# Block-0 modulation slabs by VectorE and TensorE instead of a ring and GpSimd, plain fp32 slabs for the convolution, output tile by tile

## What is computed

```python
mod = c_act @ w_ada[l] + b_ada[l]                 # 1024 x 6144 weights, one row of input
sh1, sc1, g1, sh2, sc2, g2 = jnp.split(mod, 6, axis=-1)
mix = token_mixer(modulate(x, sh1, sc1), ...)
x = layer_norm(DEEPNORM_ALPHA * x + g1[:, None, :] * mix, ln1_g[l], ln1_b[l])
ff = swiglu(modulate(x, sh2, sc2), w_gate[l], w_up[l], w_down[l])
x = layer_norm(DEEPNORM_ALPHA * x + g2[:, None, :] * ff, ln2_g[l], ln2_b[l])

# token_mixer
proj = h @ w_in
q, k, v, qi, ki, wi, gate_b, gate_c, hc = jnp.split(proj, offsets, axis=-1)
attn = sparse_indexer_attention(rope(q), rope(k), v, rope(qi), rope(ki), wi, 64)
attn = group_rms_norm(attn, attn_norm_g, 8)
u = gate_c * hc                                   # then a causal convolution of width 3
conv_out = group_rms_norm(gate_b * conv(u), conv_norm_g, 8)
return concatenate([attn, conv_out]) @ w_out
```

## Time and profile before

| | us |
|---|---|
| median of 3 runs | 1203.74 |
| lowest, highest | 1199.9, 1203.8 |
| the profiled execution | 1200.84 |
| its span | 1199.1 |
| PE busy | 1099.6 (92%) |
| DVE busy | 748.5 (62%) |
| ACT busy | 575.7 (48%) |
| POOL busy | 224.5 (19%) |
| mean granted clock of TensorE | 0.95 |
| end of the last out0 residual | 226.7 |

### The profile page before, as it was taken

The page is one execution under the profiler, slowest core; times in us unless marked ns, Lnnn a source line. Parts: engine busy times, 40 slices in busy tenths (PEclk is TensorE's granted clock), DMA queues, the critical chain, the costliest instruction groups (busy, mean ns, idle before and its releaser), DMA issues.

```text
span 1199.1 us, 20759 instructions
## 1 busy us (share of the span) xinstructions
PE 1099.6 (92%) x8133; PEld 1017.3 (85%) x8133; DVE 748.5 (62%) x1165; ACT 575.7 (48%) x977; POOL 224.5 (19%) x235
## 2 busy tenths in 40 slices
PE   6987575999999989998999999998997899999997
PEld 6686454799999968887999999997875599999997
DVE  5698543767775455774865565576777675655554
ACT  1554251474453446542555445465546664554452
POOL 0030202023331002101133331012220023332001
PEclk9988676989999999998999999998999999999998
DMA  9733406646655526440355545563432056554650
GB/s 352 283 145 141 175 1 211 210 155 215 226 167 164 153 71 233 157 172 1 104 182 206 195 134 172 179 233 141 141 137 75 1 182 204 176 188 124 198 193 36
DMA packets 182451, 192.78 MB, mean 161 GB/s; under 512 B 5673, under 2 KB 142162, under 8 KB 182258
## 3 DMA queue, kind: packets, MB, share of 16 engines
q1 hardware_dynamic: 181376, 191.15, 47.4%
q0 software_dynamic: 144, 0.52, 0.2%
q10 hardware_dynamic: 866, 0.21, 0.1%
HBM read 190.83 MB, written 1.05 MB: 160 GB/s over the span
## 4 chain that ended last, share of the span: by engine, by line
PE 68%; DVE 14%; ACT 7%; DMA 5%; issue 3%; POOL 2%; SPq 1%; POOLq 0%; DVEq 0%; ACTq 0%
PE gemm L1847 20%; PE gemm L1849 19%; PE gemm L1848 19%; DVE wlo L1222 4%; ACT whi L820 2%; DMA raw<-in_w_out 2%; PE gemm L1999 1%; DMA early<-in_w_ada 1%; PE aux L2252 1%; DMA raw<-in_w_in 1%; ACT raw L931 1%; POOL raw L653 1%; DMA raw<-in_gla_w_in 1%; PE aux L1962 1%; DVE xlo L1248 1%
## 5 line engine op out<-in xcount | busy, mean ns | idle before, releaser
L1222 DVE TENSOR_TENSOR wlo<-raw,whi 128x1024 fp32r<-128x1024 f32 (+2 forms) x340 | 386.7, 1185 | 135.5 <-ACT whi L820 134.9
L1847 PE MATMUL gemm<-ohi,whi 128*128 128x256 f32 x1504 | 433.7, 288 | 5.0 <-DVE olo L1248 3.8
L1848 PE MATMUL gemm<-olo,whi 128*128 128x256 f32 x1504 | 426.2, 283 | 0.0
L1849 PE MATMUL gemm<-ohi,wlo 128*128 128x256 f32 x1504 | 426.0, 283 | 0.0
L820 ACT ACTIVATE whi<-raw 128x1024 fp32r<-128x1024 f32 (+2 forms) x340 | 303.7, 961 | 95.9 <-PE gemm L1849 54.8
L1847 PEld LDWEIGHTS gemm<-ohi,whi 128*128 128x128 f32 x1504 | 289.8, 193 | 15.2 <-DVE olo L1248 6.6
L1848 PEld LDWEIGHTS gemm<-olo,whi 128*128 128x128 f32 x1504 | 290.0, 193 | 1.6 <-issue 1.2
L1849 PEld LDWEIGHTS gemm<-ohi,wlo 128*128 128x128 f32 x1504 | 289.5, 192 | 0.0
L1847 PE MATMUL gemm<-acthi,whi 128*128 128x256 f32 x528 | 147.9, 280 | 0.0
L1849 PE MATMUL gemm<-acthi,wlo 128*128 128x256 f32 x528 | 147.5, 279 | 0.0
L1848 PE MATMUL gemm<-actlo,whi 128*128 128x256 f32 x528 | 147.2, 279 | 0.0
(11 more groups left out here) (343 smaller groups left out, 1482.0 us busy)
## 6 DMA issues: line engine op xcount, KB each, us to landing
raw<-in_ffn_w_in SPq DMA_DIRECT2D x44, 1024.0 KB, 6.5
raw<-in_ffn_w_out SPq DMA_DIRECT2D x32, 704.0 KB, 5.3
raw<-in_gla_w_in SPq DMA_DIRECT2D x6, 2048.0 KB, 8.0
raw<-in_diff_w_in SPq DMA_DIRECT2D x6, 2048.0 KB, 7.8
raw<-in_w_gate SPq DMA_DIRECT2D x11, 1024.0 KB, 5.2
raw<-in_w_up SPq DMA_DIRECT2D x11, 1024.0 KB, 7.4
raw<-in_w_down SPq DMA_DIRECT2D x16, 704.0 KB, 5.4
raw<-in_w_ada SPq DMA_DIRECT2D x5, 2048.0 KB, 8.0
```

The lines of the kernel that those rows point to most:

```text
L1222: dve.tensor_tensor(wlo[hslot][:, q * w:(q + 1) * w], raw[slot][:, q * w:(q + 1) * w], whi[hslot][:, q * w:(q + 1) * w].bitcast(F32), ALU. ...
L1847: pe.matmul(dst, st_hi, mv_hi, start=start, stop=False)
L1848: pe.matmul(dst, st_hi, mv_lo, start=False, stop=False)
L1849: return pe.matmul(dst, st_lo, mv_hi, start=False, stop=stop_)
```

## The change

- The slabs `ada4` and `ada5` become part slabs like `ada7` to `ada11` (28 parts in place of 20), `ada6` is loaded whole into the place of `whi0` (`late`) when `in_q`'s tiles are done, and PE sums it by itself in 32 one-column matmuls (`columns_by_c`), eight before and 24 behind the group statistics. `scale_by_c` and `sum_slab` are gone, and with them POOL's part in the modulation.
- `in_gc`, `in_hc` and `in_gb` are "direct": eight plain fp32 matmuls a tile out of the raw slab, no halves by ACT and DVE. Their buffer is free when their four tiles are done.
- SP's order follows: parts stand between the slabs.
- DVE takes parts 4 and 5 between the score heads, 6 and 7 before the first logit, 8 to 11 in heads 0 to 3, and the rest beside `out0` and the feed-forward. The high half of the first operand moves from ACT to DVE; the residual's scaling by ALPHA, the scaling of probabilities and the copy of head pairs move from DVE to ACT. ACT and DVE wait for eight modulations before `out0`.
- At the end PE transposes a residual tile as soon as it is added, ACT copies pairs of tiles, DVE makes the last product in POOL's place and the last copy; SP stores four blocks of 256 columns.

Core of the diff:

```diff
-POOL_SLABS = (4, 5, 6)
-PART_SLABS = (7, 8, 9, 10, 11)
+PART_SLABS = (4, 5, 7, 8, 9, 10, 11)
...
-    ada = lambda i: Phase(f"ada{i}", 1, SLAB, 0, 1, by="pool" if i in POOL_SLABS else "mod", ahead=False,
-                          ring=i not in (2, 3), slot=0 if i == 0 else 1)
-    mixer = lambda name, slot: Phase(name, 1, SLAB, 4, 1, ahead=False, slot=slot)
+    ada = lambda i: Phase(f"ada{i}", 1, SLAB, 0, 1, by="mod", ahead=False, ring=i < 2, slot=i % 2)
+    direct = lambda name, slot: Phase(name, 1, SLAB, 4, 1, by="direct", ahead=False, slot=slot)
...
-        Phase("in_kv", 1, 8 * KV, 0, 1, by="kv", ahead=False, slot=0), mixer("in_q", 1), mixer("in_gc", 0), ada(4),
-        mixer("in_hc", 0), ada(5), mixer("in_gb", 0), ada(6),
-        Phase("out0", 2, SLAB, 4, 1, slot=0), *ffn(0),
+        Phase("in_kv", 1, 8 * KV, 0, 1, by="kv", ahead=False, slot=0),
+        Phase("in_q", 1, SLAB, 4, 1, ahead=False, slot=1), direct("in_gc", 0), direct("in_hc", 1), direct("in_gb", 0), ada(6),
+        Phase("out0", 2, SLAB, 4, 1, slot=1), *ffn(0),
...
+            def load_late():
+                wait(sp, tile_done, PH["in_q"].tile0 + 4)
+                for dst, src in sources["ada6"](0, late):
+                    sp.dma_start(dst, src).then_inc(late_in, 16)
+
             behind = {("ada1", 0): [load_x], ("in_q", 0): [*parts(0, 1), load_const, *parts(2, 3)],
-                      ("ada6", 0): parts(4, 5), ("gate_up0", 0): parts(6, 7), ("gate_up0", 1): parts(8, 9, 10, 11),
-                      ("gate_up0", 2): parts(12, 13), **{("gate_up0", i): parts(10 + i) for i in range(4, 10)},
-                      ("gla_z", 0): [load_gates]}
+                      ("in_hc", 0): parts(4, 5), ("in_gb", 0): [*parts(6, 7), load_late, *parts(8, 9)],
+                      ("out0", 0): parts(10, 11, 12, 13), ("gate_up0", 0): parts(14, 15),
+                      ("gate_up0", 1): parts(16, 17, 18, 19), ("gate_up0", 2): parts(20, 21),
+                      **{("gate_up0", i): parts(18 + i) for i in range(4, 10)}, ("gla_z", 0): [load_gates]}
...
-            for tt in range(TT):
-
-                sp.wait_ge(out_read, 2 * (tt + 1))
-                sp.dma_start(out[0, tt * P:(tt + 1) * P, :], tl(o_tok, tt, w=D)).then_inc(stored, 16)
-            sp.wait_ge(stored, 16 * TT)
+            rows_out = out[0].rearrange("(t p) n -> p t n", p=P)
+            for n in range(4):
+                sp.wait_ge(out_read, n + 1)
+                if n == 3:
+                    sp.wait_ge(last_read, 1)
+                sp.dma_start(rows_out[:, :, 256 * n:256 * (n + 1)],
+                             v3(o_tok[:, :], 2)[:, :, 256 * n:256 * (n + 1)]).then_inc(stored, 16)
+            sp.wait_ge(stored, 64)
```

```diff
-            def sum_slab(i):
-
-                w = raw[PH[f"ada{i}"].slot]
-                me.next(scaled_by_c)
-                me.link(pool.tensor_tensor(w[:, 0:2048], w[:, 0:2048], w[:, 2048:4096], ALU.add))
-                me.link(pool.tensor_tensor(w[:, 0:1024], w[:, 0:1024], w[:, 1024:2048], ALU.add))
-                wait(pool, mod_done, sum_free(i))
-                me.did(pool.tensor_tensor(MOD_SUM[i][:, :], w[:, 0:512], w[:, 512:1024], ALU.add), pool_summed)
...
-            def scale_by_c(i):
-
-                ph = PH[f"ada{i}"]
-                act.wait_ge(landed[ph.slot], ph.landed[0])
-                for k in range(KT):
-                    w = raw[ph.slot][:, 512 * k:512 * (k + 1)]
-                    ins = act.activation(w, w, ACT.Copy, scale=c_act[:, k:k + 1])
...
+            def scale_probabilities(i):
+                act.wait_ge(inverted, i + 1)
+                for qt, (c0, n) in enumerate(((0, P), (P, 2 * P))):
+                    ap = logit[:, 384 * (i % 2) + c0:384 * (i % 2) + c0 + n]
+                    ins = act.activation(ap, ap, ACT.Copy, scale=rsum[:, 2 * (i % 2) + qt:2 * (i % 2) + qt + 1])
+                me.did(ins, prob_ready)
+
+            def take_pair(p):
+                act.wait_ge(pv_done, 2 * p + 2)
+                me.did(act.activation(tl(mixed, p), X[2][:, 0:T], ACT.Copy), attn_ready)
+
...
-                if i in (0, 1):
-                    split_all("in_gb", "in_gc", range(2 * i, 2 * i + 2))
-                if i == 2:
-                    scale_by_c(5)
                 if i in (4, 5):
-                    split_all("out0", "in_hc", range(2 * i - 8, 2 * i - 6))
+                    split_all("out0", None, range(2 * i - 8, 2 * i - 6))
...
+                if i in (2, 4, 6):
+                    take_pair(i // 2 - 1)
+            take_pair(3)
+            group_squares(1, attn_ready, 4)
             group_squares(3, gated_ready, 4)
             group_root(2, G[1])
             prep(order=(0, 1), free=PH["in_gb"].tile0 + 4)
-            group_squares(1, attn_ready, 4)
+            group_root(1, X[1])
             prep(order=(4, 5))
             group_root(3, X[0])
+            prep(order=(2, 3))
             prep(order=(6, 7))
-            group_root(1, X[1])
-            prep(order=(2, 3))
-            scale_by_c(6)
+            wait(act, mod_done, 8)
...
+            for n in range(4):
+                w = 256 if n < 3 else P
+                act.wait_ge(out_done, min(2 * n + 2, KT - 1))
+                act.activation(v3(o_tok[:, :], 2)[:, :, 256 * n:256 * n + w], v3(X[(n + 1) % 4][:, :], 2)[:, :, 0:w],
+                               ACT.Copy).then_inc(out_read, 1)
...
-                me.next(ohi_ready)
+                me.link(dve.tensor_copy(tl(ohi, t), tl(om, t)), ohi_ready)
...
-            me.did(dve.tensor_scalar(res[:, :], res[:, :], ALPHA, None, ALU.mult))
...
-            for q in range(4):
-                low(PH["in_gc"], At(0), q)
+            modulate_part(4)
+            modulate_part(5)
             add_heads(range(4, IH))
...
-                low(PH["in_hc"], At(0), q)
+            modulate_part(6)
+            modulate_part(7)

...
+                invert_sums(i)
                 if i + 1 < NH:
                     masked_maxima(i + 1)
-                for q in {1: (0, 1), 2: (2, 3)}.get(i, ()):
-                    low(PH["in_gb"], At(0), q)
+                if i < 4:
+                    short_conv(i)
+                    modulate_part(2 * PARTS + i)
+                else:
+                    gated_conv(i - 4)
                 for q in {5: (0, 1), 6: (2, 3)}.get(i, ()):
                     low(PH["out0"], At(0), q)
-                if i < 4:
-                    short_conv(i)
-                else:
-                    gated_conv(i - 4)
-                if i in (2, 4, 6):
-                    take_pair(i // 2 - 1)
...
-            take_pair(3)
             me.again(gated_ready)
             prep(mix_make, order=(4, 5))
+            prep(mix_make, order=(2, 3))
             prep(mix_make, order=(6, 7))
-            me.again(attn_ready)
-            prep(mix_make, order=(2, 3))
-            dve.wait_ge(mod_done, 7)
+            dve.wait_ge(mod_done, 8)
+            dve.wait_ge(res_scaled, 1)
+            me.seen(pv_done, NH)
...
+                    if k == 2 and t == KT - 1:
+                        dve.wait_ge(ple_sig, 2 * KT)
+                        me.link(dve.tensor_tensor(tl(prod, t % 2), tl(sg, t % 2), tl(pp, t), ALU.mult))
+                    else:
+                        me.next(ple_prod)
...
             ffn(2)
             ple(2)
-            for n in range(4):
-                me.next(out_done)
-                me.did(dve.tensor_copy(tl(o_tok, n, w=512), G[n][:, :]), out_read)
+            dve.wait_ge(out_done, KT)
+            dve.tensor_copy(v3(o_tok[:, :], 2)[:, :, D - P:D], v3(G[0][:, :], 2)[:, :, 0:P]).then_inc(last_read, 1)
...
+            def columns_by_c(i, src, ks, first, last):
+
+                for k in ks:
+                    for m in range(4):
+                        ins = pe.matmul(X[3][:, 4 * i + m:4 * i + m + 1], src[:, 512 * k + P * m:512 * k + P * (m + 1)],
+                                        c_act[:, k:k + 1], start=k == first and m == 0, stop=k == last,
+                                        skip_group_check=True)
+                return ins
...
+                if not ph.split:
+                    if t == 0:
+                        pe.wait_ge(landed[ph.slot], ph.landed[0])
+                    w = flat(ph.slot, KT, 512)
+                    banks.claim(G[t], freed)
+                    for k in range(KT):
+                        ins = pe.matmul(G[t][:, 0:T], w[:, k, t * P:(t + 1) * P], tl(om, k), start=k == 0, stop=k == KT - 1)
+                    ins.then_inc(tile_done, 1)
+                    return
...
-            modulation(7)
+            modulation(4)
...
-                    modulation(4)
+                    modulation(5)
                 if i == 5:
-                    modulation(5)
+                    modulation(7)
...
+            pe.wait_ge(late_in, 16)
+            columns_by_c(6, late, range(0, 2), 0, None)
+            group_stats((1, 3), C("blk"), mix_sq, (X[1], X[0]))
```

(14 more changed lines are left out.)

79 lines of the change are left out of this document (32 added, 47 removed).

## The result

The changed kernel takes 1184.02 us (median of four runs, 1181.6 to 1185.81) against 1202.57 (four runs) for the kernel before on the same chip: a ratio of 0.984 with the interval 0.982 to 0.986, 18.6 us less. Forecast were 8 us less (1196), with a range that began at 1184: the direction was right, the size was under half of what came.

The account below looks back on a forecast made before the run. The stage up to out0's end was taken as bound by waits. Its − 5 and the tail's − 3 sum to − 8 us: 1193 from the profiled 1200.8, 1196 against the median 1203.7; range 1184 to 1208.

Parts of the forecast that it names:

- The chain of waits: Up to out0's end: DVE waits for parts 6 and 10, and PE's ada6 sum replaces 21 us ahead of out0.
- second stop: In heads 2 and 3, DVE needs parts 10 and 11, issued behind out0's slab: + 4 to + 9, 8 us taken.
- serial line: Ahead of out0, ACT scaling ada6, POOL summing it, then out0's second slab, 173.1 to 194.2 us: these 21 us go.
- parts land early: Rival, chance 0.20: loads share bandwidth and parts come with their slabs, first logit at 97, total 1184 to 1188 us.
- the price of a plain fp32 tile: In in_gc, in_hc and in_gb, a plain tile takes 8 × 0.53 = 4.2 us, against 2.8 for a split one.
- First logit: Start of the heads, 97.2 us before: a DVE wait for parts 6 and 7 puts it at about 103.
- Heads: First logit to in_gb's last tile, 64.4 us before: + 11 − 4.7 − 12 + 8 gives 67, ending at 170.
- Last in_gb tile to last residual: Up to out0's last residual, 64.6 us before: 13 + 1.5 + 35.4 = 50, ending at 220, plus 1.7 added.
- The gate's addition and the warm-up: Between PE's ada6 sum and out0's first tile: 1.5 us.
- the 4.6 us for the lower clock: In out0, two of eight tiles at the lower clock take some 2.3 us more each, added to 8 × 3.85.
- the 1.7 for a standstill: At out0's start, 1.7 us added as three engines start from standstill and ACT has the second slab's high halves first.
- Tail: Behind the last product, fewer late transposes, a smaller copy and DVE's product save 3.5, stores ± 0.5: − 3 us.

Follow-up runs that it names:

- the two runs: Changed kernel with the output written as before: 1188.1 us, 3.8 slower; kernel before with only the new output part: 1199.0 us, 4.1 faster.
- the doubled tiles: Changed kernel with the four plain tiles of one slab computed twice, a run each for in_gc, in_hc and in_gb: 1196.7, 1195.5 and 1197.0 us.

## Why the prediction was wrong

**The chain of waits was right, step by step; three sizes in it were wrong.** `allow` was freed of POOL and of no use, since DVE then waits for part 6: forecast wait 8 to 12 us, measured 8.3. There was a second stop at part 10, no serial line ahead of out0, no POOL row between 80 and 187 us, and the end was 3 us shorter. The parts landed behind their slab, 8.9 us after in_gb's issue, forecast 10. The rival "parts land early" gives the right total, but for a reason that did not occur. The sizes that failed are the price of a plain fp32 tile (4.2 us forecast, 3.46 to 3.65 measured), the second stop (8 forecast, 14 measured), and the start and speed of out0.

**First logit, 103 forecast, 99.8 measured.** PE began in_gc at 73.9, forecast 74. The term is the plain tile: 4 × 0.75 = 3.0 us too much. What else was off cancels: the load took 1.1 less than forecast, DVE's work on the two parts 1.1 more. I divided in_kv's 16.8 us by its 32 matmuls and took the mean for the price of a 128-wide one, though a quarter of them load 40 columns. The Trainium skill, FP8 and Floating Point Precision, section TensorE Precision Notes, gives four passes for true FP32; the estimate from that, with the split tile's measure, is 3.75 us, and the traces have 3.46 to 3.65. I had written that by it the forecast would be lower and kept the row: the page was nearer. Two smaller readings were off without effect on the sum: the top-k began at 72.7, not at 75, hidden behind the wait for part 6; and 406 GB/s is not the best of the earlier trace rows, which shows 417.

**Heads, 67 forecast, 62.5 measured**, and that agreement is in part luck, since two errors offset each other. Without the second stop the heads take 48.3 us (the run with parts 10 and 11 early); the forecast had 59 for that. 4.4 of the 10.7 are the tile's price. The rest, 6, I put down, without a run for it, to work of ACT and DVE that the change took out of the heads (in_gb's halves, the waits behind ada5) and to the lower clock behind the old stop, of which I took only the idle time; the runs don't separate these, and the probabilities are not among them. Against that the stop itself cost 14 to 16 us, not 8, since I let a head cover some of it and left out the clock behind it: PE stood for 11.7 us and then lost 3.1 at half the clock.

**Last in_gb tile to last residual, 51.6 forecast, 47.0 measured.** PE's sum of ada6 ended 13.2 us after the tile, as forecast. Then three terms were off. The gate's addition and the warm-up took 4.0 us, not 1.5. Out0's tiles took 29.8 us from the first matmul (179.5) to the last residual (209.3), not 35.4: in this execution the clock was full from the first of them on, behind the warm-up, so the 4.6 us for the lower clock did not come, and a tile took 3.7, not 3.85. And the 1.7 for a standstill had nothing behind it and nothing came of it.

Summed: 3.2 + 4.5 + 4.6 = 12.3 us too little gain in the stage, all three in one direction. The 4.6 and the 1.7 us were added to be careful, the tile's price was a misreading, and all made the forecast slower; the range should have reached lower.

**Tail.** − 3 forecast, − 2.9 in the trace, 3.8 and 4.1 in the times of the two runs and 3.0 and 2.5 in their traces.

## What to carry to other kernels

A mean over a group of unequal instructions is no price for one of them: look for the rows in a stretch where only the wanted kind runs, or take the shapes apart. A stop of PE costs more than its idle time, because the work behind it starts at 1.2 GHz; here 12.7 us of DVE's waiting, 11.7 of PE's, cost 14 to 16. When small loads stand behind a large one whose issue hangs on a late reader, ask whether they need to: moving two pairs of 512 KB loads by a line, with the late slab behind the first pair, gave about as much again as the whole change (20.7 and 18.6 us). And where two traces begin a stage 3 us apart, compare distances inside them: by distances the doubled tiles cost their whole length, which the times left open.

## What was not expected of the hardware

- A weight load of 40 columns made its matmul record cost 0.375 us where a load of 128 columns has 0.216.
- The clock fell from full to half while PE did one-column matmuls without a break (1.00, 0.58, 0.50 in successive stretches). Two fp32 matmuls of 512 columns, 3.8 us, ran at half the clock, and 1.2 us behind them it was full.
- Behind a like stop the first plain tile took 4.80 us in one execution and 6.31 in another, where it takes 3.65 at full clock.
- An fp32 DVE addition of two SBUF tiles (128x384) took 1.51 us instead of 0.56 beside one POOL product that began 0.2 us before it; it ended 0.4 us after POOL's. The Trainium skill, SBUF — State Buffer, section Terms, says of the port pair shared by VectorE and GpSimd that the loser "fully blocks"; the row agrees, as do `allow`'s 3.75 and 2.63 us beside POOL and 0.36 and 0.56 without it.
